# A fused diffusion-backbone layer: one convolution tap issued before the modulation product, and a finished chunk's statistics, shift and transposes moved within a scan step

## What is computed

```python
ada = jax.nn.silu(cond) @ p['w_ada'] + p['b_ada']           # modulation, 6 x 1024
sh1, sc1, g1, sh2, sc2, g2 = jnp.split(ada, 6, axis=-1)
h = modulate(layer_norm(x), sh1, sc1)
proj = h @ p['w_in']                                        # pool input, q, k, v, o, gates
qk = silu(dwconv1d_centred(concat([q, k]), w_qk_conv))      # 3 taps along the tokens
# mLSTM, chunk by chunk, forward and backward; carry C (state), n, m
s = einsum('bhtd,bhsd->bhts', qb, kb) * d
num = a_inter * (qb @ C) + s @ vb
den = a_inter * (qb @ n) + s.sum(-1)
h = num / maximum(abs(den), exp(-m_t))
C_new = decay * C + einsum('bhs,bhsd,bhse->bhde', w, kb, vb)
# then h = h_fwd + h_bwd, a layer norm of h within each head, out = sigmoid(o) * h
# concat([pool_out, out]) @ w_out, residual, norm, and a ConvFFN
```

## Time and profile before

| | |
|---|---|
| median of 3 runs | 1315.55 us (1314.51 to 1316.22) |
| the profiled execution | 1315.18 us |
| its span in the trace | 1313.4 us |
| PE busy | 1256.8 us, 96% |
| DVE, POOL, ACT busy | 77%, 49%, 44% |
| mean granted TensorE clock | 0.993 |

### The profile page before, as it was taken

How to read it: one execution, slowest core, us unless ns; L and a number is a source line. 1 busy time by engine, 2 the same in 40 slices (tenths; PEclk the granted TensorE clock), 3 DMA queues, 4 the chain that set the end, 5 groups by cost and what they waited for, 6 DMA issues and landing times.

```text
span 1313.4 us, 21580 instructions
## 1 busy us (share of the span) xinstructions
PE 1256.8 (96%) x7631; PEld 1143.5 (87%) x7631; DVE 1010.4 (77%) x1554; ACT 581.5 (44%) x1014; POOL 648.7 (49%) x519
## 2 busy tenths in 40 slices
PE   6999999999998899989999999999999999999996
PEld 3488898999987778888999999999999988888885
DVE  6466787855567698879887878787875789889898
ACT  5634013444445834555444444444443455345430
POOL 1002999404343011329878888788877864200011
PEclk9999999999999999999999999999999999999998
DMA  9534242553325532203364536354543669946892
GB/s 358 159 92 125 69 120 65 165 164 81 88 74 193 193 113 97 81 33 106 111 193 131 183 111 202 131 170 132 183 142 133 205 232 371 350 136 190 296 317 107
DMA packets 161778, 210.27 MB, mean 160 GB/s; under 512 B 10567, under 2 KB 98723, under 8 KB 161443
## 3 DMA queue, kind: packets, MB, share of 16 engines
q1 hardware_dynamic: 161214, 204.47, 47.7%
q0 software_dynamic: 288, 4.72, 0.9%
q10 hardware_dynamic: 197, 0.06, 0.0%
HBM read 161.49 MB, written 47.72 MB: 159 GB/s over the span
## 4 chain that ended last, share of the span: by engine, by line
PE 51%; POOL 2%; DVE 1%; issue 1%; ACT 0%; POOLq 0%
PE ps L1650 11%; PE ps L1648 11%; PE ps L1649 11%; PE ps L1681 6%; PE ps L1683 6%; PE ps L1682 6%; POOL tlo L2316 0%; POOL ulo L2316 0%; POOL xlo L2316 0%; POOL dwlo L2316 0%; POOL xwlo L2316 0%; PE ps L1184 0%; POOL wsum L2512 0%; DVE z L3335 0%; DVE z L3334 0%
## 5 line engine op out<-in xcount | busy, mean ns | idle before, releaser
L3149 DVE SCALAR_TENSOR_TENSOR ps<-gs,taps,ps 128x945 f32<-128x945 f32 (+2 forms) x176 | 215.7, 1226 | 10.0 <-ACT ps L2094 4.6
L2454 POOL TENSOR_TENSOR rstd<-mv,neghalf 128x1 f32<-128x1 f32 x27 | 25.1, 929 | 258.1 <-DVE mv L3326 156.9
L1277 PE MATMUL ps<-h1hi,whi 128*128 128x384 f32 x336 | 119.8, 356 | 3.8 <-DVE qk L2801 2.8
L1681 PE MATMUL ps<-dwhi,uhi 128*128 128x512 f32 x290 | 113.1, 390 | 1.2 <-POOL dwlo L2316 1.2
L1277 PE MATMUL ps<-h1hi,wlo 128*128 128x384 f32 x336 | 113.5, 338 | 0.0
L1277 PE MATMUL ps<-h1lo,whi 128*128 128x384 f32 x336 | 113.3, 337 | 0.0
L1683 PE MATMUL ps<-dwhi,ulo 128*128 128x512 f32 x290 | 112.9, 389 | 0.0
L1682 PE MATMUL ps<-dwlo,uhi 128*128 128x512 f32 x290 | 112.9, 389 | 0.0
L2316 POOL TENSOR_TENSOR wlo<-raw,whi 128x512 fp32r<-128x512 f32 x40 | 55.3, 1385 | 99.3 <-ACT whi L1753 64.5
L1648 PE MATMUL ps<-thi,xhi 128*128 128x288 f32 x320 | 94.3, 295 | 1.9 <-issue 1.1
L1650 PE MATMUL ps<-thi,wlo 128*128 128x288 f32 x320 | 94.4, 295 | 0.0
(11 more groups left out here) (453 smaller groups left out, 4000.8 us busy)
## 6 DMA issues: line engine op xcount, KB each, us to landing
raw<-in_w_up SPq DMA_DIRECT2D x78, 256.0 KB, 4.7
u_rows<-val SPq DMA_DIRECT2D x22, 576.0 KB, 2.9
adaw<-in_w_ada SPq DMA_DIRECT2D x24, 512.0 KB, 3.9
st<-in_w_down SPq DMA_DIRECT2D x22, 512.0 KB, 4.3
t_rows<-st SPq DMA_DIRECT2D x11, 1024.0 KB, 4.6
raw<-in_w_in SPq DMA_DIRECT2D x40, 256.0 KB, 4.1
w_raw<-in_w_down SPq DMA_DIRECT2D x33, 256.0 KB, 5.6
v_raw<-u_rows SPq DMA_DIRECT2D x33, 256.0 KB, 5.4
```

The lines of the kernel that those rows point to most:

```text
L1277: last = mm(ps[:, bank, 0:GN], a[:, n % 2, k * P:(k + 1) * P], b[:, kk, grp(g)], start=(kk == 0 and a is whi and b is h1hi), stop=(kk == K ...
L1681: mm(out, u_hi, w_hi, start=start, stop=False, skip_group_check=True)
L2454: tt(rstd[:, j % 4, :], mv[:, j % 4, 1:2], neghalf[:, 0, :], ALU.pow).then_inc(rstd_ready, 1)
L3149: step(stt(a3[:, ro, co], g3[:, ri, ci], taps[:, tap:tap + 1], a3[:, ro, co], ALU.mult, ALU.add), 2 + m)
```

## The change

Three orders are rewritten, and nothing is added to or taken from the work. In VectorE's projection loop, in the even turns from n = 18 on, the third tap's `conv(j, 1)` is issued before the turn's `ada_unit`s and no longer after them. In the scan steps that finish two chunks, VectorE makes the second chunk's statistics before `num_evac(s, 0)`, and both shifts between `num_evac(s, 0)` and `num_evac(s, 1)`; ScalarE makes both `h_norm` after `kw_make(s, 1)` and `d_exps(s + 1, 1)`; PE does the second `h_transposes` before `updates(s, 0)` in steps 5 and 6.

```diff
--- before.py
+++ after.py
@@ -1489,10 +1489,12 @@
                 for ck in done[:1]:
                     h_transposes(ck)
                 o_slot(s, "c")
-                if s != LT - 1:
+                if s == LT:
                     updates(s, 0)
                 for ck in done[1:]:
                     h_transposes(ck)
+                if s < LT - 1:
+                    updates(s, 0)
             assert not o_groups
             updates(LT, 1)
 
@@ -2010,12 +2012,10 @@
                 kw_make(s, 0)
                 if s + 1 < NSTEP:
                     d_exps(s + 1, 0)
-                for _ in done[:1]:
-                    h_norm()
                 kw_make(s, 1)
                 if s + 1 < NSTEP:
                     d_exps(s + 1, 1)
-                for _ in done[1:]:
+                for _ in done:
                     h_norm()
                 for _ in done:
                     h_evac()
@@ -2868,10 +2868,12 @@
                     gate_chain4()
                 if n == 9:
                     gate_chain5()
+                if n > V_LAST and n % 2 == 0:
+                    conv((n - 1) // 2 - 2 * H, 1)
                 for unit in range(ada_done(n - 1), ada_done(n)):
                     ada_unit(unit)
-                if n > V_LAST:
-                    conv((n - 1) // 2 - 2 * H, (n + 1) % 2)
+                if n > V_LAST and n % 2:
+                    conv((n - 1) // 2 - 2 * H, 0)
             conv(2 * H - 1, 1)
             dve.wait_ge(pe_ada, N_ADA1 + N_ADA2)
             link(ada_evac(6, A_G1, A_G2))
@@ -2988,20 +2990,13 @@
                 p_make(s, 1)
                 if 1 <= s < LT:
                     u_add(s - 1, 1)
+                done = [ck for at, ck in final if at == s - 1]
+                for _ in done[1:] if s < LT else ():
+                    h_stats()
                 num_evac(s, 0)
-                done = [ck for at, ck in final if at == s - 1]
-                if s < LT:
-                    for _ in done[:1]:
-                        h_shift()
-                    for _ in done[1:]:
-                        h_stats()
-                    num_evac(s, 1)
-                    for _ in done[1:]:
-                        h_shift()
-                else:
-                    for _ in done:
-                        h_shift()
-                    num_evac(s, 1)
+                for _ in done:
+                    h_shift()
+                num_evac(s, 1)
                 if s < LT - 1 or s == LT:
                     u_add(s, 0)
                 done = [ck for at, ck in final if at == s]
```

## The result

The changed kernel takes 1306.18 us in the median of 5 runs (1304.43 to 1307.85), the one before 1316.22 in as many runs of its own; the ratio is 0.9929, with a 95% interval of 0.9909 to 0.9950. That is 10.0 us, or 0.7%, and the forecast was 1305.0 against 1315.5. The profiled execution took 1306.18 us, 9.0 less than that of before.

A forecast was written before the change was run, and what follows sets the result against it. PE is busy 96% of the span, so only its waits or clock count. 2.84 + 1.4 + 0.3 + 2.0 + 0.6 + 3.3 = 10.4 us off 1315.18 gives 1304.8, stated as a median of 1305.0, range 1302.8 to 1309.3.

The forecast's parts named there:

- The taps, -2.84: Projection, turns 22 and 24: PE's waits of 2.28 and 0.56 us for VectorE's last tap go; delayed modulation units cost nothing.
- Step 5, -1.4: Scan step 5: waits of 1.91 and 0.78 us go, new ones of 0.4, 0.4 and 0.5 come; bounds -2.2 and -0.6.
- My reading of the earlier trace: Scan, VectorE's numerators: a small SBUF instruction under POOL's Qa product is held, making updates wait another 0.4 us.
- Step 6, -0.3: Scan step 6: waits of 1.98 us go, 1.3 comes back, 0.4 is paid for statistics in step 7.
- Steps 7 and 8, -2.0 and -0.6: Scan end: step 7's waits of 0.49 and 1.47 go, 0.78 stays; step 8 loses 0.45 and a little more.
- The scan in all: Scan steps 5 to 8 without the clock: 1.4, 0.3, 2.0 and 0.6 us, 4.3 us of waits gained.
- The clock, -3.3: Scan, behind the waits of steps 5 and 7: both falls of PE's clock go, winning 3.3 us; bounds 0 and 3.3.
- the clock does not come back: Scan: falls stay or come elsewhere, 1308.3 us, or 1306.6 with one fall of two; chance 0.24.
- slower: Steps 5 and 6: VectorE waits through POOL for a Qa transfer of 8.7 us, giving 1315.6 or 1318.9; chance 0.05.
- The shift's wait eats the gain: Steps 5 and 6: late POOL or Qa holds VectorE's second shift; 1309.8 us, or 1311.9 with steps 7 and 8; chance 0.09.

The follow-up runs named there:

- x3: The change, with both of POOL's powers of a step issued ahead of both selects, no longer behind the wait for Qa; 1304.37 us, ratio 0.9912 to before.
- x1: The kernel before with only the tap's move in VectorE's projection loop, scan orders old; 1309.15 us, ratio 0.9945 to before.
- x4: The change with PE's old order, updates(s, 0) ahead of the second chunk's transposes in steps 5 and 6; 1304.82 us, ratio 0.9917 to before.
- x7: The change with VectorE's scan order of before, PE's and ScalarE's orders staying new; 1311.81 us, ratio 0.9978 to before.
- x5: The change with statistics of a step's own first finished chunk made behind VectorE's first shift, not at the step's end; 1302.88 us, ratio 0.9898 to before.
- x2: The change with the tap's move undone, so only the new scan orders; 1310.16 us, ratio 0.9958 to before.
- x8: The change with ScalarE's scan order of before; 1306.51 us, ratio 0.9944 to before.

## Why the prediction was right, and where its steps were not

**The taps, -2.84: the mechanism right, the size 3.7.** Two things were missed. The idle time in a row starts where the last matmul is reckoned to end; between starts, PE lost 214.51 - 211.89 - 0.17 = 2.45 us at the 2.28 us of the earlier trace rows, since matmuls run 0.17 apart there, and 0.73 at the 0.56. And a third wait, 0.27 us before turn 20, was too short to be listed. Together 3.45 of 3.68. What was put off, the modulation units, cost nothing, as forecast.

**Step 5, -1.4: it gave -0.7.** The new wait came in the form that was forecast. VectorE and POOL in step 5 of the change, against the earlier trace rows:

```profile
376.29 0.58 DVE L2983 SCALAR_TENSOR_TENSOR nmh<-mvh,rsh 128x4 f32<-128x4 f32 x1 [3.85 <-POOL rsh L2443]
...
377.82 1.24 DVE L2921 TENSOR_TENSOR hacc<-hacc,tmph 128x256 f32<-128x256 f32 x1
...
379.68 0.42 DVE L2919 TENSOR_TENSOR tmph<-ps,rden 128x256 f32<-128x256 f32 x1
```

```profile
374.01 1.26 POOL L2419 TENSOR_TENSOR Qa<-Qa,qk 128x512 f32<-128x512 f32 x1 [6.61 <-DMA Qa<-scan_rows]
375.23 1.02 POOL L2443 TENSOR_TENSOR rsh<-mvh,neghalf 128x4 f32<-128x4 f32 x1
376.21 0.65 POOL L2412 TENSOR_SCALAR_AFFINE_SELECT Dm<-Dm 128x512 f32<-128x512 f32 x1
```

The second shift stands 3.85 us for POOL's power, which stands behind the product that waits for Qa. Two sizes were off. The shift itself took 0.58 us and not 0.16, while POOL's select (376.21 to 376.86) ran; I had no row for that. And the sum at 377.82, two SBUF tensors, took 1.24 us where 0.42 is usual: it ran on 0.3 us past the end of POOL's second product (377.50 to 378.78). The wait for the updates was 0.49, for 0.4 forecast, and that before the transposes 0.79, for 0.4. x3 undoes both and gains 0.9 to 1.9 us over both steps.

My reading of the earlier trace rows, that any small SBUF instruction under such a product is held, did not stand. VectorE in step 6, under POOL's product of 395.93 to 397.20:

```profile
396.13 0.17 DVE L2912 RECIPROCAL rden<-rden 128x2 f32<-128x2 f32 x1
...
396.79 0.69 DVE L2921 TENSOR_TENSOR hacc<-hacc,tmph 128x256 f32<-128x256 f32 x1
397.79 1.12 DVE L2935 SCALAR_TENSOR_TENSOR Cs<-Cs,decb,ps 128x129 f32<-128x129 f32 x4 [0.31 <-PE ps L1449]
398.84 0.86 DVE L2969 BATCH_NORM_STATS2 sth<-hacc 128x6 f32<-128x128 f32 x4
...
400.24 1.29 DVE L2894 SCALAR_TENSOR_TENSOR Dm<-ps,Dm 128x512 f32<-128x512 f32 x2
401.44 1.12 DVE L2935 SCALAR_TENSOR_TENSOR Cs<-Cs,decb,ps 128x129 f32<-128x129 f32 x4
```

The reciprocal at 396.13, one SBUF input, ran in 0.17 us. In the same stretch the sum of two SBUF tensors was stretched (0.69 for 0.42), and updates(6, 0) did not wait for the numerators at all. This agrees with GPSIMD Engine Reference of the Trainium skill, section "Key points", which names instructions in a 2-port mode or with two SBUF inputs. The instruction that was held in the earlier trace rows reads one SBUF tensor; by that rule it ran in a 2-port mode, which no row here can show.

**Step 6, -0.3 (bounds -1.3 and +0.4): it gave about +1.0 against the trace of before, and this is the step that failed.** From the first transposes of step 6 to the numerators of step 7 it was 407.53 - 399.26 = 8.3 us before, and 402.71 - 393.49 = 9.2 now. The prediction said of the 1.4 us of statistics in step 7 that "PE's earlier start and VectorE's short waits swallow 1.0". What is late is something else, and the rows above show it: VectorE adds updates(6, 0) at 397.79, makes the statistics of step 6's own first chunk at 398.84, the two products at 400.24, and only at 401.44 adds updates(6, 1), for which the numerators of step 7 wait. That is a string of 4.9 us of VectorE from 397.79 to 402.71. It starts with updates(6, 0), and it was there before, as PE's rows in that trace show:

```profile
401.81 1.05 PE L1449 MATMUL ps<-v,kw 128*128 128x129 f32 x8
...
407.53 0.46 PE L1433 MATMUL ps<-v,Dm 128*128 128x129 f32 x2
```

| kernel | first transposes of step 6 | updates(6, 0) | numerators of step 7 | between the last two | idle before these |
|---|---|---|---|---|---|
| before | 399.26 | 401.81 | 407.53 | 5.72 | none |
| x1 (old scan) | 395.06 | 397.61 | 404.49 | 6.88 | none |
| x4 (PE old) | 393.98 | 397.14 | 402.90 | 5.76 | 0.90 |
| x7 (DVE old, PE new) | 395.00 | 399.98 | 405.53 | 5.55 | 2.07 |
| x3 (early shift) | 393.43 | 396.42 | 402.05 | 5.63 | 2.07 |
| the change | 393.49 | 397.06 | 402.71 | 5.65 | 2.08 |
| x5 (statistics out) | 393.58 | 396.89 | 401.13 | 4.24 | 0.67 |

The 5.72 us of before and the 5.65 of the change are as good as equal (in x1 PE's own longer wait of 2.03 us set the 6.88). So the waits of 0.86, 0.78 and 0.34 us, which the prediction counted as gained, lay beside VectorE's string, and their going gave nothing against that trace. The wait of 2.07 comes with PE's new order, which puts the second transposes ahead of updates(6, 0) and leaves PE less to do behind them; it is the same with VectorE's old order (x7) and with an early shift (x3). What the change lost is the later start of updates(6, 0): 3.6 us behind the first transposes, 3.0 in x3 and 2.6 before. So the late shift has 0.6 of the 1.0, and the second transposes, now ahead, about 0.4. x5 takes 1.4 us out of the string and gets 1.4 us of the wait.

The trace of before flatters the old kernel here, though. Its fall behind step 5 hid 1.2 us of step 6's first wait, as x1 shows. Against x1, where the step took 9.4 us, the change gave -0.2 and x2, with 9.0, -0.5: near the forecast, but by two errors against each other, a wait of 2.07 where 0.4 was put, and old waits that were 1.2 longer than in the earlier trace rows.

**Steps 7 and 8, -2.0 and -0.6: right in sum.** From the numerators of step 7 to the gate broadcast x1 took 27.2 us with one fall in it, x2 22.5 with none; less 1.7 for the fall that is 3.0, for 2.6 forecast. x8 gives ScalarE's share (0.49, 0.45 and some I had not counted), and x7 shows 1.86 us for the second norm without VectorE's new order.

**The scan in all:** 4.3 us of waits forecast; 4.5 measured, x1 against x2, and 3.6 in the traced run of the change against that of before. In x1 against x2, steps 5 and 6 gave 1.5 of the 1.7 forecast and the end of the scan 0.4 more; in the change steps 5 and 6 gave only 0.6.

**The clock, -3.3: half of it in the traced run.** One of the two falls went and one moved behind the new wait of step 7: -1.7. The prediction counted both falls in full beside the waits, but where the fall behind step 5 is gone, 1.2 us of step 6's wait come back (x1), so the two terms weren't independent. Over the runs the mean clock went from 0.9927 (18 runs) to 0.9948 (5), which is 2.8 us of the span. That this is the scan's new order isn't shown: x1, with the old one, has 0.9942, x2 0.9943, and x7 and x8 0.9933 and 0.9934. So the first rival, "the clock does not come back", was true in part in the traced run, and whether 3.3 was right on average stays open. In which run a fall comes is not the kernel's alone: the head is the same in all ten kernels, and the clock fell behind 44 us in five of their traces; x2 and the change have one scan order, and it fell in the scan only in the change. TensorE: Matmul & The Clock Gate of the Trainium skill (Part 1, "The HAM clock gate") has the look at activity run freely against the kernel's start, and these traces fit that.

**The sum, and its luck.** From trace to trace the taps gave 3.7 us, the scan's waits 3.6 and the clock 1.7, 9.0 in all, where 2.84, 4.3 and 3.3 were forecast, 10.4. The medians moved by 10.0. That the total came within 1.2 us of the forecast owes something to the taps, whose surplus of 0.8 made up for a third of what the other two fell short.

**The rivals.** Qa landed as before (median 3.6 us, longest 9.1), so "slower" did not come; but the wait that it was built on is the one x3 found, and with POOL's product 0.4 us later in step 5 the change lost 0.6 us there against x2. "The shift's wait eats the gain" was true in part: it ate 0.9 to 1.9 us.

## What to carry to other kernels

When an order is changed so that one engine is no longer late, look at once for the longest string of work on the other engines between the same two points: it was hidden by as much as the first was late, and it is the next bound (here 4.9 us of VectorE). Before a small instruction is moved ahead on one engine, ask what the engine that feeds it waits for in its own queue; here a 1 us power stood behind a transfer, and moving the power was worth 0.9 to 1.9 us, beside 4.5 for the whole reordering of the scan. A wait that ends may have run beside another engine's longer work, and then its going gives nothing (step 6). And compare such changes by stages of the trace, since falls of the clock, which come and go between runs at up to 1.7 us each, are as large as what is measured.

## What the runs showed of the hardware

- A fall of TensorE's granted clock to half took 1.7 us of clock each time (1.68 to 1.72 in twelve that lie apart), at places where PE waits, but not at the same ones in each run: behind 44 us in five of ten traces, behind step 5 in one, in step 7 or 8 in five, in the projection in one. Through a wait of 2.28 us in a busy stretch the full clock held in one trace (before, window 212 to 216 at 1.00) and not in another (x2, the same window at 0.69).
- A fall hides part of the wait behind it, so subtracting it from the time gives too little: x1 against before, 135.2 and 134.1 us for the same scan. The fall in step 7 of the change and of x3 cost that stage 0.6 us (23.1 against 22.5 in four kernels without it).
- A VectorE instruction with two SBUF inputs was slowed under POOL's select, which has one tensor in, as under its product: the second shift took 0.58 us in the change, and 0.16 in x8, where the select came later (376.02, the shift at 375.37).
